# The gated delta rule in chunks of 128 tokens instead of 64, with the levels of its triangular inverse spread over quarters of token tiles

## What is computed

```python
def gated_delta_rule_chunked(q, k, v, g, beta):
    C = GDN_CHUNK                       # 64
    gcum = jnp.cumsum(gc, axis=-1)      # within a chunk
    decay = jnp.where(causal, jnp.exp(gcum[..., :, None] - gcum[..., None, :]), 0.0)
    a_strict = jnp.where(strict, jnp.einsum('bnhid,bnhjd->bnhij', kc, kc) * decay * bc[..., :, None], 0.0)
    rhs = jnp.concatenate([vc * bc[..., None], kc * (bc * jnp.exp(gcum))[..., None]], axis=-1)
    sol = triangular_solve(a_strict + jnp.eye(C), rhs, left_side=True, lower=True, unit_diagonal=True)
    u, w = sol[..., :dv], sol[..., dv:]
    qk = jnp.einsum('bnhid,bnhjd->bnhij', qc, kc) * decay
    q_dec = qc * jnp.exp(gcum)[..., None]
    k_dec = kc * jnp.exp(g_last[..., None] - gcum)[..., None]
    def step(state, xs):
        v_new = u_n - w_n @ state
        o_n = q_n @ state + qk_n @ v_new
        state = state * jnp.exp(gl_n) + k_n.T @ v_new
        return state, o_n
```

## Time and profile before

| | |
|---|---|
| median of 3 runs | 2107.82 us (2106.69 to 2108.97) |
| the profiled execution | 2106.81 us, span 2105.0 us |
| PE busy | 2067.5 us, 98% of the span |
| DVE / ACT / POOL busy | 1537.3 / 1026.8 / 89.3 us |
| mean granted clock of PE | 0.997 |

### The profile page before, as it was taken

How to read it: one execution, slowest core, us unless ns; L and a number is a source line. 1 busy time by engine, 2 the same in 40 slices (tenths; PEclk the granted TensorE clock), 3 DMA queues, 4 the chain that set the end, 5 groups by cost and what they waited for, 6 DMA issues and landing times.

```text
span 2105.0 us, 27045 instructions
## 1 busy us (share of the span) xinstructions
PE 2067.5 (98%) x9802; PEld 1719.1 (82%) x9802; DVE 1537.3 (73%) x2414; ACT 1026.8 (49%) x1281; POOL 89.3 (4%) x98
## 2 busy tenths in 40 slices
PE   8999999999999999999999999999999999999998
PEld 6888887888788888788888879878888888878887
DVE  6787766877678766687778867547876887676876
ACT  5445554444444555444454447535445444555443
POOL 1000100000100010000010000210001000020000
PEclk9999999999999999999999999999999999999999
DMA  7554534555654453455564543315455555434552
GB/s 289 212 188 165 195 140 147 195 205 196 229 213 179 175 186 140 156 195 205 197 215 180 183 157 141 119 40 200 179 196 193 211 197 190 162 111 168 186 206 106
DMA packets 54003, 376.14 MB, mean 179 GB/s; under 512 B 6528, under 2 KB 6672, under 8 KB 9264
## 3 DMA queue, kind: packets, MB, share of 16 engines
q1 hardware_dynamic: 51120, 364.93, 47.6%
q0 software_dynamic: 2528, 10.22, 1.6%
q10 hardware_dynamic: 288, 0.07, 0.0%
HBM read 374.15 MB, written 1.05 MB: 178 GB/s over the span
## 4 chain that ended last, share of the span: by engine, by line
PE 90%; DVE 4%; ACT 3%; DMA 1%; issue 1%; POOL 0%; POOLq 0%; ACTq 0%; DVEq 0%; SPq 0%
PE bank L1509 27%; PE bank L1511 27%; PE bank L1510 27%; DVE w_lo L929 1%; DMA w_raw<-weights_dram 1%; PE bank L1518 1%; ACT w_hi L460 1%; PE bank L1712 1%; PE bank L1697 0%; DVE mix L1072 0%; DVE mix L981 0%; PE bank L1915 0%; PE bank L1926 0%; PE bank L1873 0%; ACT xn L473 0%
## 5 line engine op out<-in xcount | busy, mean ns | idle before, releaser
L929 DVE TENSOR_TENSOR w_lo<-w_raw,w_hi 128x2048 fp32r<-128x2048 f32 x344 | 786.8, 2291 | 264.2 <-ACT w_hi L460 168.0
L1509 PE MATMUL bank<-w_hi,xt_hi 128*128 128x512 f32 x1888 | 746.7, 396 | 10.5 <-DVE w_lo L929 6.6
L1511 PE MATMUL bank<-w_hi,xt_lo 128*128 128x512 f32 x1888 | 736.6, 390 | 0.0
L1510 PE MATMUL bank<-w_lo,xt_hi 128*128 128x512 f32 x1888 | 735.6, 390 | 0.0
L532 ACT ACTIVATE w_hi<-w_raw 128x2048 fp32r<-128x2048 f32 x192 | 366.5, 1910 | 131.0 <-PE bank L1511 131.0
L1509 PEld LDWEIGHTS bank<-w_hi,xt_hi 128*128 128x128 f32 x1888 | 354.9, 188 | 85.6 <-DVE w_lo L929 9.2
L1511 PEld LDWEIGHTS bank<-w_hi,xt_lo 128*128 128x128 f32 x1888 | 354.6, 188 | 75.2
L1510 PEld LDWEIGHTS bank<-w_lo,xt_hi 128*128 128x128 f32 x1888 | 355.1, 188 | 71.3
L981 DVE STREAM_TRANSPOSE mix<-hid 32x128 f32<-32x128 f32 x1152 | 349.0, 303 | 17.2
L460 ACT ACTIVATE w_hi<-w_raw 128x2048 fp32r<-128x2048 f32 x152 | 290.5, 1916 | 113.6 <-PE bank L1511 100.5
L1509 PE MATMUL bank<-w_hi,ht_hi 128*128 128x512 f32 x672 | 263.3, 392 | 2.8 <-DVE ht_lo L1394 1.5
(11 more groups left out here) (259 smaller groups left out, 1442.3 us busy)
## 6 DMA issues: line engine op xcount, KB each, us to landing
w_raw<-weights_dram SPq DMA_DIRECT2D x345, 1024.0 KB, 4.8
mix<-a_b_gate_dram POOLq DMA_DIRECT2D x4, 1024.0 KB, 15.3
mix<-a_pool_mean_dram POOLq DMA_DIRECT2D x2, 768.0 KB, 6.3
x<-x_dram SPq DMA_DIRECT2D x4, 256.0 KB, 7.0
w_raw<-weights_dram SPq DMA_DIRECT2D x4, 256.0 KB, 5.2
out_dram<-xn SPq DMA_DIRECT2D x2, 512.0 KB, 2.6
mix<-a_pool_w_dram POOLq DMA_DIRECT2D x2, 256.0 KB, 3.6
mix<-g_ret_dram POOLq DMA_DIRECT2D x1, 512.0 KB, 7.1
```

What stands on the lines that cost most here:

```text
L929: nc.vector.tensor_tensor(w_lo[s][:, :], w_raw[s][:, :], w_hi[s][:, :].bitcast(F32), ALU.subtract).then_inc(lo_done, 1)
L1509: nc.tensor.matmul(out, a_hi, b_hi, start=start, stop=False)
L1510: nc.tensor.matmul(out, a_hi, b_lo, start=False, stop=False)
L1511: return nc.tensor.matmul(out, a_lo, b_hi, start=False, stop=stop)
```

## The change

A chunk is 128 tokens, so there are two, each one token tile. One state step is left between them. The inverse needs one level more (l = 6, six in this form), and level 5 must now produce the inverse as well as its transpose. The decays across half chunks (`sub`) go; q with decay, and w, are needed for the second token tile only. On PE small blocks of pieces 10 to 13 move from after a token tile to after each quarter of a piece (`quarter(p, tt, end)`, after 6 and after 12 matmuls of a token tile). The retention scores go to banks 0 and 1 and their outputs to banks 2 and 3, where they used 6 and 7. The cut diff:

```diff
-                for l in range(1, 6):
+                for l in range(1, 7):
...
                 def square_output(tt):
-                    act.wait_ge(M["o_done"], 2 * tt + 2)
+                    act.wait_ge(M["o_done"], tt + 1)
...
-                        scale_in_place("kb_kbe", e4[:, 0:8], "kbe_ready")
+                        scale_in_place("kb_kbe", 1, e4[:, 0:8], "kbe_ready")
+                        scale_in_place("k_kd", 0, e4[:, 8:16], "kd_ready")
                     if p == 11:
+                        take_t1(3)
                         take(k, 5, tok(G["rg"]), ACT.Silu, 3)
-                        take_t1(3)
-                        scale_in_place("k_kd", e4[:, 8:16], "kd_ready")
...
                     if p == 13:
+                        take_t1(5)
+                        take_t1(6)
                         take(k, 6, tok(G["gz"]), ACT.Silu, 3)
-                        take_t1(5)
...
                     if p == 14:
-                        next_state(0)
-                        for n in range(1, 4):
-                            new_values(n)
-                            if n == 2:
-                                output_mean(0)
-                            if n < 3:
-                                next_state(n)
+                        first_state()
+                        output_mean(0)
+                        new_values()
+                        norm_output(0)
                         ahead(n0 + 14)
-                        norm_output(0)
...
-                    consts = (G["before"], G["after"], G["sub"][:, 0:P], G["sub"][:, P:2 * P])
-                    for i, m in enumerate(consts):
+                    for i, m in enumerate((G["before"], G["after"])):
...
-                            if l < 5:
+                            if l < 6:
                                 mm(bank[6 + tt][:, cols], inv_t[:, tt, h, :], prod1[:, tt, h, :], start=True, stop=True)
...
+                def per_head_1(out, lhs, rhs, start):
+
+                    for h in range(4):
+                        ins = mm(out[:, h * P:(h + 1) * P], lhs(h), rhs(h), start=start and h == 0, stop=True, skip_group_check=True)
                     return ins
...
+                def first_tile():
+
+                    per_head_1(bank[5], lambda h: kd[:, 0, h, :], lambda h: uu[:, 0, h, :], True).then_inc(M["ds_done"], 1)
+                    per_head_1(bank[6], lambda h: qk_m[:, 0, h, :], lambda h: uu[:, 0, h, :], True).then_inc(M["o_done"], 1)
+
+                def second_tile_state():
+
+                    pe.wait_ge(M["s_ready"], 1)
+                    per_head_1(bank[4], lambda h: wt[:, h, :], lambda h: state[:, h, :], True).then_inc(M["vw_done"], 1)
+                    per_head_1(bank[7], lambda h: qdt[:, h, :], lambda h: state[:, h, :], True)
+
+                def second_tile_own():
+
+                    pe.wait_ge(M["vn_ready"], 1)
+                    per_head_1(bank[7], lambda h: qk_m[:, 1, h, :], lambda h: v_new[:, h, :], False).then_inc(M["o_done"], 1)
...
+                def quarter(p, tt, end):
+
+                    at = (p, 2 * tt + end)
+                    if at == (10, 1):
+                        pe.wait_ge(M["tm_ready"], 3)
+                        level_b(1)
+                    if at == (10, 2):
+                        pe.wait_ge(act_evac, e0 + 4)
+                        retention_scores(0)
+                        retention_scores(1)
+                    if at == (10, 3):
+                        level_a(2)
+                    if at == (11, 0):
+                        level_b(2)
+                    if at == (11, 1):
+                        retention_scores(2)
+                        retention_scores(3)
+                    if at == (11, 2):
+                        level_a(3)
+                    if at == (11, 3):
+                        level_b(3)
+                    if at == (12, 1):
+                        level_a(4)
+                    if at == (12, 2):
+                        level_b(4)
+                    if at == (12, 3):
+                        retention_outputs()
+                    if at == (13, 0):
+                        level_a(5)
+                    if at == (13, 1):
+                        level_b(5)
+                    if at == (13, 2):
+                        level_a(6)
+                    if at == (13, 3):
+                        level_b(6)
...
-                        own_values(0)
-                    elif slot < 7:
-                        (old_values if slot % 2 else own_values)((slot + 1) // 2)
-                    elif slot == 7:
+                        first_tile()
+                    if slot == 1:
+                        second_tile_state()
+                    if slot == 2:
+                        second_tile_own()
+                    if slot == 5:
                         pe.wait_ge(M["half_normed"], 3)
                         turn_pair(tok(G["decay_oa"]), 0, 4)
-                    elif slot == 8:
+                    if slot == 6:
                         turn_pair(tok(G["decay_oa"]), 2, 5)
```

More of the change, by code:

```diff
@@ L1640, in chunk_piece @@
                                     up_view(w_hi[s], q), up_view(w_lo[s], q), kt == 0, kt == KT - 1)
+                        if quarter and q == 1:
+                            quarter(tt, 0)
                     if half == 1 and tt == 0:
@@ L2014, in hook @@
                         pe.wait_ge(M["qd_ready"], 1)
-                        turn_heads(tok(G["q_qd_u"]), 6).then_inc(M["qdt_turned"], 1)
+                        for h in range(4):
+                            ins = nc.tensor.transpose(bank[6][:, h * P:(h + 1) * P], tok(G["q_qd_u"])[:, 1, h * P:(h + 1) * P], ident[:, :])
+                        ins.then_inc(M["qdt_turned"], 1)
                     if p == 9 and tt == 0:
@@ new lines, in retention_outputs @@
+                def retention_outputs():
+                    pe.wait_ge(act_evac, e0 + 6)
+                    pe.wait_ge(M["rs_ready"], 4)
+                    for h in range(4):
+                        pr, cols = retention_probs(h), slice(h * P, (h + 1) * P)
+                        mm(bank[2][:, cols], pr[:, 0:P], rv[:, 0, h, :], start=True, stop=True)
+                        mm(bank[3][:, cols], pr[:, P:2 * P], rv[:, 0, h, :], start=True, stop=False)
+                        ins = mm(bank[3][:, cols], pr[:, 2 * P:3 * P], rv[:, 1, h, :], start=False, stop=True)
+                    ins.then_inc(M["ro_done"], 1)
@@ L2301, in delta_ret_constants @@
     i, j = np.arange(P)[:, None], np.arange(P)[None, :]
-    same = i // 64 == j // 64
     f = lambda m: np.asarray(m, np.float32)
-    levels = [f((i >> (l + 1) == j >> (l + 1)) & ((i >> l) % 2 == 0) & ((j >> l) % 2 == 1)) for l in range(6)]
+    levels = [f((i >> (l + 1) == j >> (l + 1)) & ((i >> l) % 2 == 0) & ((j >> l) % 2 == 1)) for l in range(7)]
     gamma = 1.0 - 2.0 ** (-5.0 - np.arange(4, dtype=np.float64))
@@ L2308, in delta_ret_constants @@
     ret = [f(np.where(d >= 0, g ** np.maximum(d, 0), 0.0)) for g in gamma]
[L2309 to L2311 removed]
+    return {"g_ones": f(np.ones((P, P))), "g_before": f(i <= j), "g_after": f(i > j),
+            "g_below": f(np.where(i <= j, 0.0, NEG)), "g_level": np.concatenate(levels, 1),
             "g_ret": np.concatenate(ret, 1), "g_rope": rope_table(64), "g_zeros": np.zeros((P, 12), np.float32)}
```

141 lines of the change are left out of this document (44 added, 97 removed).

## The result

The changed kernel takes 2100.12 us (median of 8 runs, 2097.64 to 2102.05), the kernel before 2106.98 (8 runs, 2103.81 to 2108.97). The ratio is 0.9965, with a 95% interval of 0.9956 to 0.9974: 7.4 us less, between 5.5 and 9.3 (the two medians lie 6.9 apart). Forecast was 2101.8 in a range of 2099.0 to 2105.0, and faster. The profiled execution took 2102.05 us, span 2100.2, so by the two profiles alone the gain is 4.8.

A forecast was written before the change was run, and what follows sets the result against it. The prediction took PE (TensorE), busy for 98% of the span, as the bound. Its terms, -0.4 -0.4 -0.9 +5.4 +0.5 -9.2 -1.0, summed to -6.0 us: median 2101.8 us, range 2099.0 to 2105.0.

The forecast's parts named there:

- Fewer turns of q: On PE, four of eight turns (transposes) of the decayed q go: -0.4 us.
- Level 6: On PE in the level stretch, 48 more records at 0.112 us, including level 5's update of the inverse: +5.4 us.
- Interruptions: PE, pieces 10 to 13: six more returns from small blocks to weight matmuls at 0.08 us each: +0.5 us.
- State steps: On PE, 104 records taking 14.4 us become 40 in three slots taking 5.2: -9.2 us.
- The waits: PE before the output's turns: two waits costing 3.9 us become one of 2.9, behind ACT's high split: -1.0 us.
- The chain between the levels: ACT, POOL and DVE work between level halves keeps up with PE: costed at nothing, bound one low split, 2.2 us.
- part 1: On PE, two sums of decays go (-0.4 us), four turns of q (-0.4) and half the w products (-0.9).
- The clock: Granted clock behind PE's wait before the output: falling to 0.50 as before held a bit likelier; otherwise -1.5 us more.
- the forecast's branch: Whole kernel: terms as summed and the clock falls as before, -6.0 us; chance 0.47.
- the second case: Whole kernel: the clock stays up behind the one wait before the output, -7.5 us; chance 0.30.
- the smaller gain: State slots' extra doesn't go with the records (+2.0), or level chain misses by a split (+2.2): about -4.0 us; chance 0.18.
- The slower one: Weight splits get ahead of the level chain at every level and hold PE: total +12 us; chance 0.05.

The follow-up runs named there:

- Experiment 1: Changed kernel with ACT's squares of the second token tile's output ahead of the high split of piece 17; 2095.83 us, ratio 0.9941 to the kernel before.
- experiment 2: Changed kernel with its level blocks put back after whole token tiles; 2099.77 us, ratio 0.9964 to the kernel before.
- experiment 3: Changed kernel without level 6, level 5 making only the transpose (inverse incomplete); 2094.26 us, ratio 0.9940 to the kernel before.
- experiment 4: Changed kernel with the output's two turn pairs put back after slots 7 and 8; 2098.05 us, ratio 0.9957 to the kernel before.
- experiment 5: Changed kernel with state products of slots 0 and 2 summed over the first 64 tokens only; 2099.45 us, one run.
- experiment 6: Changed kernel with squares before piece 17's split, POOL's first mask released earlier, piece 15's high split moved into step 12; 2094.22 us, ratio 0.9942 to before.

## Why the prediction was right

Its mechanism and sign held, and the median lies 1.7 us below the number given. By its steps:

1. *Fewer turns of q*, -0.4: from the turns at 1294.55 (now 1296.06) to piece 10 it was 35.39 us, now 35.36, of which 0.43 more are the first mask's wait. So PE had 0.46 less to do, and lost nearly all of it again: the mask ends 33.5 us behind these turns in both traces (1328.08 and 1329.56), and PE only came to it sooner. The sums of decays lie in the phase's opening, where the granted clock is 0.50 for nearly 7 us in either trace, at times that differ, and can't be read there to 0.4 us: in the kernels that are the same up to piece 10 (the changed one and experiments 1 to 5) the first stretch takes 76.56 to 78.97 us.
2. *Level 6*, +5.4: experiment 3 measured 5.3.
3. *Interruptions*, +0.5: this term was wrong, they cost 0. A block of 16 with its return takes 1.79, and 16 x 0.112 is 1.79. In the earlier trace rows it shows too, had I added up: the first weight matmul starts 3.49 us after the block's first record, 0.08 before 32 x 0.112 = 3.57 are over, and the one behind it 0.08 late. I took the block at 3.57 and the 0.08 besides, so the return was counted twice.
4. *State steps*, 5.2: measured 4.47. I took the level product's 0.112 for the record, which is right, and added 0.25 a slot, a number that no row gave. Experiment 5 shows that the extra comes with half-array products between whole ones; the new slots have none. The change is -9.9 and not -9.2.
5. *The waits*, 3.9 to 2.9: PE lost 2.96, through the chain that was written down (split, squares, mean, power, scaling). Experiment 1 shows its cause. The second wait went, and came back in experiment 4 as soon as the turns were late again.
6. *The chain between the levels*, 0: the two places named as tight were the two that slipped, level 5's second half by 0.28 us, and level 3's first half by some 0.12 (its 16 records take 2.07 at 1352.24, elsewhere 1.95). The bound of a whole split was not reached. What I missed is the first mask, +0.43: the walk began behind it. Of the w products, -0.9 in part 1, the trace shows -1.1: from the turns of the retention outputs to piece 14 it was 4.53 us (from 1380.26), now 3.47 (from 1387.38).
7. *The clock*: it fell behind the one wait, as held likelier, and this profile therefore agrees with the forecast's branch. But experiments 2 and 3, with the same wait of 2.80 and 2.81 us, kept it at 1.00. So the two first cases of the prediction were not two answers of which one is true: the kernel has both, by the execution.

Summed with what was measured (the sums of decays as predicted): -0.4 -0.5 -1.1 +5.3 +0 -9.9 -0.9 +0.4 +0.4 = -6.7 us (sums, turns, w, level 6, interruptions, state, waits, the two tight places, first mask), where the phase shows -7.1. I can't assign the 0.4 between them.

Part of the agreement in the total is luck: interruptions, state steps and w were forecast 1.4 us too dear together, and 0.8 us of lost time in the level stretch and at the mask was put at nothing. And the median fell by 6.9 us, nearer to the -7.5 of the second case than to the -6.0 of the forecast.

The gap that the Trainium skill gives (TensorE: Matmul & The Clock Gate, Back-to-back issue gap: about 81 ns, total near -3.1) does not fit: the 48 records of experiment 3 cost 0.111 each, and the block of 16 here 0.112.

The rivals: the smaller gain had two legs, and both were tried. The extra of the slots went with the half-array form (shown by experiment 5 for 64 rows), and the chain missed by tenths, not by a split. The slower one needed weight splits ahead of every level; even experiment 2, with less room than the change, shows only 0.48 and 0.73 us.

What stays open: how often the clock falls behind this wait. Eight runs of the changed kernel spread over 4.4 us, which is more than one fall's 1.55, and one profile for each kernel can't say which run had which. Another source is the opening of the phase, where the first stretch differs by up to 2.4 us between profiles of the same code, with the granted clock at 0.50 for 3.4 us (experiments 3 and 5) to 10.2 us (1 and 4).

## What to carry to other kernels

When a product ends earlier than before, look at what stands ahead of its consumer in the consumer's queue: work that used to be done long before (here a weight split, 11 us ahead) may now be released later than the product, and must be put behind it. Price a small block from the first weight matmul before it to the second one after it, so that the return is counted once. And count changes of the array's shape, not only records: whole-array products spared 0.3 to 0.5 us a slot besides the records.

## What the runs showed of the hardware

**The clock behind the same wait differs from run to run.** Behind the wait of 2.8 us it fell to 0.50 in the changed kernel and in experiment 5, not in 2 and 3. Behind the wait of 2.05 us at 573.83 (for a low split, far ahead of the change) it fell in the changed kernel:

```profile
573.83 0.53 PE L1504 MATMUL bank<-w_hi,xt_hi 128*128 128x512 f32 x1 [2.05 <-DVE w_lo L933]
```

```profile
574.00:575.00 1.00, 1.00 (x3) 0.77 (x4) 1.00 (x2) 1.00 (x2) 0.00 (x0) 0.58 0.47 66
575.00:576.00 1.00, 1.00 (x4) 0.80 (x3) 1.00 (x1) 0.81 (x1) 0.00 (x0) 0.50 0.34 90
576.00:577.00 1.00, 1.00 (x4) 0.81 (x3) 1.00 (x2) 0.00 (x0) 0.00 (x0) 0.50 1.05 442
```

In the kernel before, the same wait (2.07 us at 573.48) left it at full speed. At this place and at the one of the earlier trace rows the eight profiles hold seven waits of 2.01 to 2.07 us. Behind four of them the clock fell (at 573.83 in the changed kernel, 572.66 in experiment 3, 48.44 in 5, 48.36 in 4), behind three it didn't (573.48 and 48.42 in the kernel before, 48.65 in the changed one). So the wait of the earlier trace rows that passed unpunished is punished in other executions. The wait's length differs too: at 573 it is 0.55 to 0.96 us in the other five profiles. This one fall is about 1.6 of the 2.1 us by which this profile is longer ahead of the phase, and so may be most of why the two profiles show 4.8 us and the medians 6.9.

**POOL and DVE hold each other up.** POOL's mask takes 2.38 to 2.41 us at five levels, and 3.87 (before the change 3.38) at the first, where DVE has two low splits on from 1322.85 to 1327.33:

```profile
1325.69 3.87 POOL L388 TENSOR_TENSOR mix<-xn,mix 128x1024 f32<-128x1024 f32 x1 [21.59 <-ACT mix L645]
1331.75 2.41 POOL L388 TENSOR_TENSOR mix<-xn,mix 128x1024 f32<-128x1024 f32 x1 [2.19 <-PE bank L1914]
```

From DVE's end at 1327.33, 2.4 us lead to 1329.7, and the mask ended at 1329.56: it looks as if it had done nothing until then. Before the change DVE ended at 1325.83, the mask at 1328.08, again 2.25 later. In experiment 6 the mask ran earlier, beside other DVE work, and there both paid:

```profile
1307.61 3.42 POOL L388 TENSOR_TENSOR mix<-xn,mix 128x1024 f32<-128x1024 f32 x1 [6.61 <-DVE xn L1153]
```

```profile
1307.56 1.22 DVE L1159 TENSOR_TENSOR mix<-xn,mix 128x1024 f32<-128x1024 f32 x1
1308.82 3.29 DVE L1160 TENSOR_TENSOR mix<-ident,mix 128x1024 f32<-128x1024 f32 x1
```

The same DVE instruction (L1160 here) takes 1.23 us in the changed kernel, without POOL beside it. The ends stand in a row, as if the engines took turns: DVE's first ends at 1308.78, the mask 2.25 later at 1311.03, DVE's second 1.08 after that. The Trainium skill (SBUF — State Buffer, Terms) says that the two share one pair of ports, which one holds for a full instruction while the other is blocked. The traces agree in the ends, to some 0.2 us; no run here separates the port from another cause.
